# Block inverse of a gated delta rule on four quadrants of TensorE, with small products in row and column strips

## The reference

```python
kb, vb = k * beta[..., None], v * beta[..., None]
decay = exp(where(causal, g[..., :, None] - g[..., None, :], -inf))
Lmat = where(strict, einsum('bhncd,bhnmd->bhncm', kb, k) * decay, 0.0)
rhs = concatenate([vb, kb * exp(g)[..., None]], axis=-1)
sol = triangular_solve(Lmat, rhs, left_side=True, lower=True, unit_diagonal=True)
```

```python
a_gate = h @ w_in[l][:, gate columns]        # 24 columns
ga = sigmoid(a_gate)
```

## Time and profile before

| what | value |
|---|---|
| median of 3 runs | 4115.61 us (4114.34 to 4120.4) |
| the profiled execution | 4117.21 us |
| its span in the trace | 4115.3 us |
| PE, DVE, ACT, POOL busy | 97%, 51%, 20%, 32% of the span |
| mean granted clock of PE | 0.981 of full |
| heads stage | about 92 to 340 us |
| five levels of the inverse | 346 to 419 us |
| last level, up to the values | 419 to 452.7 us |
| attention's start, first and second layer | 1793 and 2954 us |

### The profile page before, as it was taken

The page is one execution under the profiler, slowest core; times in us unless marked ns, Lnnn a source line. Parts: engine busy times, 40 slices in busy tenths (PEclk is TensorE's granted clock), DMA queues, the critical chain, the costliest instruction groups (busy, mean ns, idle before and its releaser), DMA issues. The chain is left out here.

```text
span 4115.3 us, 56239 instructions
## 1 busy us (share of the span) xinstructions
PE 3986.3 (97%) x20987; PEld 3126.9 (76%) x20987; DVE 2093.4 (51%) x3932; ACT 817.2 (20%) x1835; POOL 1301.6 (32%) x1027
## 2 busy tenths in 40 slices
PE   7998999999999999999999999999999999999998
PEld 3887768887886688866688648888666787478887
DVE  3777434323553433125548436884354485257852
ACT  2342210002333100004411202111133301011110
POOL 1333024444220244431146101544311372004543
PEclk8999899999999999999999999999999999999999
DMA  7222134325441223251223231332532233313232
GB/s 243 72 61 97 52 109 125 89 85 142 139 120 40 77 82 92 85 120 44 65 75 83 72 102 50 84 91 85 107 68 65 53 84 82 92 41 92 82 87 77
DMA packets 623012, 360.79 MB, mean 88 GB/s; under 512 B 68778, under 2 KB 592459, under 8 KB 622324
## 3 DMA queue, kind: packets, MB, share of 16 engines
q1 hardware_dynamic: 607944, 335.62, 30.1%
q10 hardware_dynamic: 14892, 22.78, 1.7%
HBM read 344.18 MB, written 6.82 MB: 85 GB/s over the span
## 5 line engine op out<-in xcount | busy, mean ns | idle before, releaser
L849 PE MATMUL psum<-h_normed,weight_slot 128*128 128x256 f32 x2624 | 594.9, 380 | 0.0
L849 PEld LDWEIGHTS psum<-h_normed,weight_slot 128*128 128x128 f32 x2624 | 499.3, 190 | 69.5 <-issue 1.4
L757 POOL TENSOR_TENSOR weight_slot<-weight_slot 128x512 f32<-128x512 f32 (+1 forms) x130 | 168.1, 1293 | 880.4 <-DMA weight_slot<-in_w_ffn_in 292.4
L949 DVE COPY work<-psum 128x256 f32<-128x256 f32 x98 | 41.2, 421 | 592.0 <-PE psum L849 592.0
L3596 PE MATMUL psum<-sums_of_h,weight_slot 128*128 128x256 f32 x1280 | 282.8, 379 | 0.0
L3596 PEld LDWEIGHTS psum<-sums_of_h,weight_slot 128*128 128x128 f32 x1280 | 243.2, 190 | 33.1
L849 PE MATMUL psum<-sums_hidden,weight_slot 128*128 128x256 f32 x1056 | 243.6, 379 | 0.0
L849 PE MATMUL psum<-sums_in,weight_slot 128*128 128x256 f32 x1008 | 231.3, 379 | 0.0
L4488 DVE SCALAR_TENSOR_TENSOR u<-raw,vectors,u 128x511 f32<-128x511 f32 (+1 forms) x160 | 200.0, 1270 | 61.2 <-ACT u L4460 49.5
L849 PE MATMUL psum<-sums_of_h,weight_slot 128*128 128x256 f32 x960 | 221.1, 380 | 4.6 <-POOL weight_slot L763 4.6
L849 PEld LDWEIGHTS psum<-sums_hidden,weight_slot 128*128 128x128 f32 x1056 | 200.6, 190 | 27.3
(11 more groups left out here) (599 smaller groups left out, 7032.6 us busy)
## 6 DMA issues: line engine op xcount, KB each, us to landing
weight_slot<-in_w_ffn_in SPq DMA_DIRECT2D x88, 512.0 KB
weight_slot<-in_ffn_w_up SPq DMA_DIRECT2D x88, 512.0 KB
weight_slot<-in_w_gate SPq DMA_DIRECT2D x64, 512.0 KB
weight_slot<-in_w_in SPq DMA_DIRECT2D x40, 512.0 KB, 5.5
weight_slot<-in_dsw_w_in SPq DMA_DIRECT2D x36, 512.0 KB, 6.6
weight_slot<-in_gdn_w_in SPq DMA_DIRECT2D x32, 512.0 KB, 14.5
weight_slot<-in_w_ffn_out SPq DMA_DIRECT2D x64, 256.0 KB
tile_ahead<-in_w_ada SPq DMA_DIRECT2D x16, 1024.0 KB, 5.3
```

The source lines that it names most:

```text
L757: nc.gpsimd.tensor_tensor(b(self.S1), b(self.A21), b(self.A22), ALU.add).then_inc(self.folded, 1)
L849: last = nc.tensor.matmul(c.ps[:, 4 * bank + r // 2, (r % 2) * self.HALF:(r % 2 + 1) * self.HALF], c.slots[s][:, b * 512 + k * P:b * 512 + ...
L949: nc.vector.tensor_copy(u4, p(self.P1)).then_inc(self.link, 1)
```

## The change

Three things are rearranged; the results are the same functions of the inputs.

In the inverse, T stays on its half of the partitions and U moves to the other: U of the block on partitions 0 to 63 now comes from partitions 64 to 127 and the other way round. So the triangle in `lt` is written with its halves exchanged (the end of `gdn_heads`), the inner product goes across the array, and the outer products of one step use all four 64x64 quadrants: two crossing ones into one bank, two straight ones into the next. They are issued alternately, a chunk at a time. A step's outer products have two pairs of banks instead of four banks. The turns now make T and U both by a matmul (16 matmuls instead of 8) and ACT copies both. DVE's subtraction is the same single instruction in all five levels; putting U into `full` is now two copies by ACT in the last level, with a new semaphore `widened`. The eight rows of the fourth modulation tile go from DVE to GpSimd, as 8 products and 7 sums, after its masks; the rows of the other three (24) start after step 1 and are spread over 36 steps. `sum_tiles` moves from the last level to behind the first values. SP's next loads also wait for the last outer products and for `widened`.

In the rows and heads stages, beta gets a second place on partitions 32 to 39, so that the products that spread G and beta stand on different strips of rows. The head's pick is written twice.

In `attend`, gate weights are padded to 32 columns and the 8 gate products go to four column strips, two each. The four partial sums are copied without the sigmoid and are turned by a matmul with a constant (`gatefold`) that adds them; ACT takes the sigmoid after that.

```diff
             act.wait_ge(beta_ready, 1)
-            nc.scalar.activation(stacked[32:32 + GH, :], decay_rows[:, B, :], ACT.Copy).then_inc(rows_stacked, 1)
+            nc.scalar.activation(stacked[32:32 + GH, :], decay_rows[0:GH, B, :], ACT.Copy).then_inc(rows_stacked, 1)
+            nc.scalar.activation(decay_rows[BETA_ROWS, B, :], decay_rows[0:GH, B, :], ACT.Copy)
...
-                pe.wait_ge(picked, n + 1)
+                pe.wait_ge(picked, n * 2 + 2)
                 pe.wait_ge(rooted, n * 2 + 1)
-                for r, bank in ((G, 6), (B, 4)):
-                    last = nc.tensor.matmul(c.ps[:, bank, :], picks[:, s, :], decay_rows[:, r, :], start=True, stop=True)
+                for r, bank, at in ((G, 6, slice(0, GH)), (B, 4, BETA_ROWS)):
+                    last = nc.tensor.matmul(c.ps[:, bank, :], picks[at, s, :], decay_rows[at, r, :], start=True, stop=True)
                 last.then_inc(spread, 1)
...
-                nc.scalar.activation(picks[:, s, :], c.ones[0:GH, :], ACT.Copy, scale=hot[:, ds(n, 1)]).then_inc(picked, 1)
+                for at in (slice(0, GH), BETA_ROWS):
+                    nc.scalar.activation(picks[at, s, :], c.ones[at, :], ACT.Copy, scale=hot[at, ds(n, 1)]).then_inc(picked, 1)
...
-        PAIRS_AHEAD, ADA_FROM, ADA_SLOTS = 3, 4, 40
+        PAIRS_AHEAD, ADA_FROM, ADA_SLOTS = 3, 1, 36
+        POOL_ROW = ADA_LATE - 1
...
             sp.wait_ge(taken, 2 * ADA_LATE)
-            sp.wait_ge(x_done, (LAST + 1) * GH)
+            sp.wait_ge(yz_done, (LAST + 1) * GH)
+            sp.wait_ge(widened, GH)
...
+            to = scaled[:, POOL_ROW, :]
+            for k in range(KT):
+                half, at = k // (KT // 2), k % (KT // 2)
+                row, col = tile[:, half, at, :], c.cond[:, k:k + 1]
+                if at == 0:
+                    pool.wait_ge(half_loaded[half], ADA_LATE * 16)
+                nc.gpsimd.tensor_scalar(row if k else to, row, col, None, ALU.mult).then_inc(pool_link, 1)
+                if k:
+                    pool.wait_ge(pool_link, 2 * k)
+                    nc.gpsimd.tensor_tensor(to, to, row, ALU.add).then_inc(pool_link, 1)
+                if at == KT // 2 - 1:
+                    pool.wait_ge(pool_link, 2 * k + 1)
+                    pool.wait_ge(taken, 2 * POOL_ROW + half)
+                    pool.sem_inc(taken, 1)
...
-                    pe.wait_ge(t_begun, h - 1)
+                    pe.wait_ge(t_begun, h)
+                first, bank = pair_of[h % 4], 4 if h == 1 else 6
                 for at in CHUNKS:
                     for b in BLOCKS:
-                        last = nc.tensor.matmul(c.ps[b, 6 + h % 2, at], tu[b, h, 1, at], c.ident[b, b], start=True, stop=True)
+                        nc.tensor.matmul(c.ps[b, bank, at], first[b, at], c.ident[b, b], start=True, stop=True)
+                    for b, other in CROSSED:
+                        last = nc.tensor.matmul(c.ps[other, bank + 1, at], c.ident[b, b], first[b, at],
+                                                start=True, stop=True)
                 last.then_inc(turned, 1)
...
-                        for b in BLOCKS:
-                            last = nc.tensor.matmul(c.ps[b, h % 2, at], mask_of[h % 4][b, at], tu[b, h, 0, at], start=True, stop=True)
+                        for b, other in CROSSED:
+                            last = nc.tensor.matmul(c.ps[b, h % 2, at], mask_of[h % 4][other, at], tu[other, h, 0, at], start=True, stop=True)
                     else:
-                        last = nc.tensor.matmul(c.ps[HC:P, h % 2, at], lower[0:HC, h, t, HC:P], tu[0:HC, h, 0, at], start=True, stop=True)
+                        last = nc.tensor.matmul(c.ps[HC:P, h % 2, at], lower[HC:P, h, t, HC:P], tu[HC:P, h, 0, at], start=True, stop=True)
                 last.then_inc(x_done, 1)
...
-                j, bank = i * GH + h, 2 + h % 4
+                j, bank = i * GH + h, 2 + h % 2 * 2
                 pe.wait_ge(x_copied, j + 1)
-                if j >= 4:
-                    pe.wait_ge(tu_ready, j - 3)
+                if j >= 2:
+                    pe.wait_ge(tu_ready, j - 1)
                 x = inner_of[h % 2]
                 if i < LAST:
                     for at in CHUNKS:
-                        for b in BLOCKS[0:1] if i == LAST - 1 else BLOCKS:
-                            nc.tensor.matmul(c.ps[b, bank, at], tu[b, h, 1, at], x[b, at], start=True, stop=True)
-                    for t, at in enumerate(CHUNKS):
+                        for b, other in CROSSED:
+                            nc.tensor.matmul(c.ps[other, bank, at], tu[b, h, 1, at], x[b, at], start=True, stop=True)
                         for b in BLOCKS:
-                            last = nc.tensor.matmul(c.ps[b, bank, W + t * HC:W + (t + 1) * HC], x[b, at], tu[b, h, 1, at], start=True, stop=True)
+                            last = nc.tensor.matmul(c.ps[b, bank + 1, at], x[b, at], tu[b, h, 1, at], start=True, stop=True)
                 else:
-                    for t, at in enumerate(CHUNKS):
-                        last = nc.tensor.matmul(c.ps[0:HC, bank, at], x[HC:P, at], full[HC:P, h, t, HC:P], start=True, stop=True)
+                    for at in CHUNKS:
+                        last = nc.tensor.matmul(c.ps[0:HC, bank, at], x[HC:P, at], tu[HC:P, h, 1, at], start=True, stop=True)
                 last.then_inc(yz_done, 1)
 
             def keys(h):
                 pe.wait_ge(tu_ready, LAST * GH + (h + 1))
+                pe.wait_ge(widened, h + 1)
...
-                if h == GH:
-                    sum_tiles()
...
+                    if n == 0:
+                        sum_tiles()
...
-                nc.scalar.activation(tu[:, h, 0, :], c.ps[:, 6 + h % 2, 0:W], ACT.Copy).then_inc(t_begun, 1)
+                nc.scalar.activation(tu[:, h, :, :], c.ps[:, 4:6, 0:W] if h == 1 else c.ps[:, 6:8, 0:W], ACT.Copy).then_inc(t_begun, 1)
...
+                    if h == 0:
+                        act.wait_ge(cleared, 1)
+                    act.wait_ge(tu_ready, (LAST - 1) * GH + (h + 1))
+                    for b in BLOCKS:
+                        last = nc.scalar.activation(full[b, h, :, b], tiles(tu[b, h, 1, :]), ACT.Copy)
+                    last.then_inc(widened, 1)
...
-                nc.vector.tensor_tensor(tiles(tu[:, h, 1, :]), levels[:, LEVELS - 1:LEVELS, :].to_broadcast([P, TT, HC]),
-                                        tiles(pair_of[h % 4]), ALU.subtract).then_inc(started, 1)
+                first = tiles(pair_of[h % 4])
+                nc.vector.tensor_tensor(first, levels[:, LEVELS - 1:LEVELS, :].to_broadcast([P, TT, HC]),
+                                        first, ALU.subtract).then_inc(started, 1)
 
             def level(i, h):
-                j, bank = i * GH + h, 2 + h % 4
+                j, bank = i * GH + h, 2 + h % 2 * 2
                 dve.wait_ge(yz_done, j + 1)
-                if i < LAST - 1:
-                    both = tu[:, h, :, :].rearrange("p a n -> p (a n)")
-                    nc.vector.tensor_tensor(both, both, c.ps[:, bank, :], ALU.subtract).then_inc(tu_ready, 1)
-                elif i == LAST - 1:
-                    nc.vector.tensor_tensor(tu[0:HC, h, 0, :], tu[0:HC, h, 0, :], c.ps[0:HC, bank, 0:W], ALU.subtract)
-                    if h == 0:
-                        dve.wait_ge(cleared, 1)
-                    for b in BLOCKS:
-                        last = nc.vector.tensor_tensor(full[b, h, :, b], tiles(tu[b, h, 1, :]), tiles(c.ps[b, bank, W:S]), ALU.subtract)
-                    last.then_inc(tu_ready, 1)
+                if i < LAST:
+                    both = tu[:, h, :, :]
+                    nc.vector.tensor_tensor(both, both, c.ps[:, bank:bank + 2, 0:W], ALU.subtract).then_inc(tu_ready, 1)
...
-            ROWS = KT * ADA_LATE
+            ROWS = KT * POOL_ROW
...
-            sp.dma_start(gate_w[:, :, :], layer_columns(w_in, layer, GATE_A, 24)).then_inc(gate_w_loaded, 16)
+            sp.wait_ge(fold_ready, 1)
+            sp.dma_start(gate_w[:, :, 0:24], layer_columns(w_in, layer, GATE_A, 24)).then_inc(gate_w_loaded, 16)
...
+            nc.gpsimd.memset(gate_w[:, :, :], 0.0).then_inc(fold_ready, 1)
+            pool.wait_ge(fold_ready, 1)
...
-                    last = nc.tensor.matmul(c.ps[0:24, 2, :], gate_w[:, k, :], c.h[:, k, :], start=(k == 0), stop=(k == KT - 1))
+                    part = slice(32 * (k % 4), 32 * (k % 4) + 32)
+                    last = nc.tensor.matmul(c.ps[part, 2, :], gate_w[:, k, :], c.h[:, k, :], start=(k < 4), stop=(k >= KT - 4))
                 last.then_inc(gates_done, 1)
 
             def turn_gates():
-                pe.wait_ge(squashed, 1)
+                pe.wait_ge(parts_copied, 1)
+                pe.wait_ge(consts, CONSTS)
                 for t in range(TT):
-                    last = nc.tensor.transpose(c.ps[:, 3, t * 24:(t + 1) * 24], gate_rows[:, t * P:(t + 1) * P], c.ident[0:24, 0:24])
```

(5 more changed lines are left out.)

62 lines of the change are left out of this document (33 added, 29 removed).

## The result

| what | value |
|---|---|
| median of 6 executions | 4096.0 us (4086.42 to 4105.01) |
| before, 6 executions | 4116.25 us |
| ratio | 0.9949 (0.9937 to 0.9961) |
| profiled execution, its span | 4087.29 us, 4085.5 us |
| mean granted clock | 0.985 (before 0.981) |

What follows compares the result with a forecast made beforehand. PE, busy 97% of the span, was taken as the bound. Gains of 6.1, 8.8, 11.1 and 16.6 less 0.6 sum to 42.0 us; 4115.6 less that gives 4074, own range 4060 to 4086, with rivals 4060 to 4098.

Steps and rivals of the forecast that it cites:

- rows, up to the first pair: Rows stage: PE waits for ACT's stacked rows, and one more beta copy ahead of them costs 0.6 us.
- heads, first pair to the levels: Heads stage: G and beta matmuls overlap on different row strips, saving 0.87 us for each of seven heads, 6.1 us.
- levels: First five levels of the inverse: four quadrants halve the outer products, DVE becomes longer, old gaps stay; 11.1 us gained.
- last level to the first turned output: Inverse's last level and values: no 3.0 us wait, clock stays at 2.4 GHz, ACT is the bound; 16.6 us gained.
- gates, start to compression, both layers: Attention in both later layers: gate products on four column strips take 1.75 us instead of 6.98; 8.8 us gained.
- my list of signs: What would show the forecast wrong, including halts much longer than 2.1 us as PE asks for instructions faster.
- PE starts 64x64 records no closer than now: Rival, 18%: records in the levels stay 29 ns apart, so levels lose 2.8 us instead of gaining 11.1; 4088.
- The rule that spoke against: Matmul starts never closer than about 25 ns; by it the levels gain 3.2 us and the kernel takes 4082.
- rival 2: Rival, 20%: the clock falls in the last level after all, nothing gained there, 17.0 us less gain; 4091.
- the 3 us wait: Old last level: PE waits 3.0 us once for DVE's backlog, with clock 0.50 behind it; forecast to go.
- GpSimd's row: Modulation products and sums moved to GpSimd, 12 to 24 us: hidden, or 1 us at the dear end.

Runs made afterwards that it cites:

- all edits: Changed kernel with wide crossing turns, tiles loaded in 256 KB pieces, second `hot` load moved later; outer products in either order: medians 4082.79, 4080.38, repeated 4082.04 us.
- pieces with constants alone: Changed kernel with tiles loaded in 256 KB pieces and the second `hot` load moved behind the other constants, without wide turns: 4080.68 us, ratio 0.9911.

## Why the prediction failed, step by step

| term | forecast | profile at 4087.3 | profile at 4096.4 |
|---|---|---|---|
| rows, up to the first pair (118.50; 121.12; 122.72) | -0.6 | -2.6 | -4.2 |
| heads, first pair to the levels (227.5; 222.0; 222.0) | 6.1 | 5.5 | 5.5 |
| levels (73.1; 73.6; 70.1) | 11.1 | -0.5 | 3.0 |
| last level to the first turned output (43.2; 29.4; 42.8) | 16.6 | 13.9 | 0.4 |
| gates, start to compression, both layers (42.6; 36.4; 34.5) | 8.8 | 6.1 | 8.0 |
| sum | 42.0 | 22.4 | 12.7 |

The spans differ by 29.8 and 20.7. The 7 to 8 us beyond the sums lie in stages that the change doesn't touch; part of them is that the profile of before had the clock down there (32 matmuls ahead of the gates took 15.84 us, after 13.90).

*The levels: this step failed.* "I keep the old gaps whole, because the halts do not come from either engine", and DVE's 47.7 with them: 47.7 + 14.2 = 61.9 was forecast, 73.6 and 70.1 were measured. The engines' times came as priced (DVE 48.4, PE at 15 ns a record). But the halts are no fixed toll on top of the longer engine: they are waits for PE's instructions, whose supply is a bound of its own. (Of the 14.2 us of gaps only 7.7 are such halts in the trace of before.) 128 records come every 3.5 us at best. Before, PE needed 3.7 us for them (1.40 for 48), just slow enough to hide most of it; the change needs about 2.5, so halts of 7.7 us became 13.9 to 16.7. At 3.5 us each 17 transfers make 60 us (an estimate), below which these levels don't come with any engine times; measured are 66.0 without tile loads and 68 to 75 with them. That PE asking faster would lengthen the halts stood in my list of signs, without a price. A rival with the right time for the levels, "PE starts 64x64 records no closer than now", was wrong in its cause: they start 15 ns apart.

*The rule that spoke against.* The Trainium skill, "TensorE: Matmul & The Clock Gate", section "Wait — 56ns, not 53.3ns?", has no start-to-start below about 25 ns; the trace shows 15 ns over 32 records on four quadrants, so the measurement decides. The Trainium skill also bears on what happened: "Runtime: NRT & Kernel Launch", section "Instruction fetch mechanics", says that instructions come in blocks of 16 KiB, 256 instructions. The trace agrees (17 transfers, 0.28 MB, 2,176 records with their loads). It says too that this is hidden, as engines dispatch slower than blocks arrive; here halts of 16.7 us in 73.6, each ending behind a transfer, say otherwise.

*The last level: right with the clock up.* 15.3 us against 16.1, ACT-bound at 1.76 a head against 1.7; column sums 4.1 against 3.4, as the clock falls within them, and the 2.4 us of values at half clock were not won, since the clock is 0.53 from 438 to 444. But rival 2, "the clock falls in the last level after all", is what happens in most executions: 8 of 12, judging by their times and mean clocks, as only two are profiled. It had 20% and 17 us; it is worth 13.5. I took the 3 us wait for the cause of the low clock; with that wait gone it still falls. What makes it fall is open: PE is idle for a sixth to a third of the levels, with and without tile loads, with two quadrants and with four, and fifteen profiles fall in two kinds, last level 15.3 (eight) or 24.4 to 24.9 us (seven). With all edits three profiles of three are of the better kind, and whether the other twelve executions are isn't shown; nor is it told apart which edit would do that, since pieces with constants alone had one of four in the other. So the good profile of the change owes its last level in part to luck: in the median execution the 16.6 us priced here were not gained.

*Heads: right, but for a transfer.* 5.5 to 6.0 against 6.1. The second load of `hot` wasn't in the sum, and costs 2.0.

*Gates: right in the mechanism.* The products take 1.9 us and the turning 0.97. The first layer gains 4.6 and 4.7 in two profiles and 2.7 in that of the change, where PE idles 1.88 us ahead of the compression, forecast 4.7; the second gains 3.4 to 3.6, forecast 4.1. "They have landed at about 2985.2" was read from the drop of the DMA share and is 1.1 us too early: the landing time is 2986.3 by the issue and its time to landing.

*GpSimd's row* was hidden: it ends at 433.3, and the sums begin at 433.85 without a wait.

## What to carry to other kernels

Where an engine runs a straight stream of tiny instructions, count the instructions and the transfers that bring them, as one more resource with its own time, before pricing a faster way to execute them. Where that resource binds, fewer instructions and less DMA beside them shortened the stretch here (60.5 and 66.0 us), and faster execution did not. Cutting the large loads into pieces is worth a try; in these runs its share was not told apart. When the times of a kernel fall in groups, profile one of each: the median can be a group that a single good profile doesn't show. A good series of four is not a finding until it has been repeated.
